# Attention layer: fill products dealt over the steps, output projection in two halves

## The chip, the cores and the metric

The kernel runs on one core of one Trainium2 chip. The metric is the device time of one execution in microseconds (us). The kernel before ran three times, at 1906.16, 1908.15 and 1908.15 us: median 1908.15 us.

## The reference

The reference is a model of four layers on 512 positions of width 1024, all in float32. The change touches only the last mixer, grouped-query attention with a window of 128 positions, 16 query heads and 4 key/value heads of 64 channels, and the residual sum behind it. `hn` and `hk` are two normalised forms of the same `h`.

```python
q = partial_rope((hn @ w_q).reshape(1, 512, 16, 64), pos)
k, v = partial_rope(hk @ w_k, pos), hk @ w_v             # 4 heads
# per kv head (4) and block of 128 queries (4): keys are this block and the one before
s = (q . k) * 64 ** -0.5, masked to the window of 128
m = max(max(s), sink); pr = exp(s - m)
w = pr / (sum(pr) + exp(sink - m)); o = w @ v
h = h + o @ w_o
h = h + square(relu(rmsnorm(h) @ w_up)) @ w_down         # MLP, 4096 wide
h = h + sigmoid(rmsnorm(h) @ w_gate) * (p @ w_proj)      # p: 512 x 256
```

## The kernel before

Every engine has its own written-out program (`pe_*` for TensorE, `dve_*` for VectorE, `act_*` for ScalarE, `pool_*` for GpSimd, `sync` for the queue SP that issues the DMAs). An engine runs its program strictly in order; semaphores tie the programs together. So the order around the change is set by hand, in `pe_att`, `act_att`, `dve_att` and `pool_att`.

All weights come in units of 128 x 1024 floats, 281 of them, in the fixed order `ORDER`. Unit i is loaded into slot i % 3 of `RAW`; ScalarE rounds it to fp32r (`high`, L276, into `WH`), GpSimd takes the remainder (`low`, L280, into `WL`). A product in full precision is three fp32r matmuls: WH by xh, WL by xh and WH by xl, where xh and xl are the rounded activations and their remainder. A unit is thus 24 matmuls of 128 x 128 by 512 (`linear`, L291, matmul on L304; for the projection of p `mm3`, L287 to L289). `high` of unit i waits until TensorE has finished unit i - 3, and `low` waits for `high`; the next fetch into a slot waits for its `low`.

The attention layer goes like this. Key and value units come first (`wk`, `wv`), then query units 0 to 4, each followed by the rotation of the one before it (`pe_rope`, L2012, between VectorE's scaling L410, its sine product L2017, GpSimd's cosine product L2024 and VectorE's sum L2030). Then 18 steps run, n = 0 to 17, with the 16 pairs of a kv head and a block in a pipeline over the engines:

- TensorE: scores of pair n+1 (`pe_scores`, L2073), output of pair n-2 (`pe_out`, L2162), transposes of the weights of pair n-1 (`pe_weights`, L2144).
- VectorE: masked scores and maxima of pair n in two halves (`dve_scores`, L2096 to L2106), the sum of pair n-1 between them (`dve_sum`, L2119, L2121), the remainder of output n-2 (`dve_out`, L417).
- ScalarE: rounding of output n-2 (`act_out`, L413), exponentials of pair n (`act_exp`, L2112, L2114), copy of the transposes of pair n-1 (`act_weights`, L2152).
- GpSimd: the division of pair n-1 (`pool_weights`, L2127).

A pair whose block is the first has 128 keys, the 12 others 256. Buffers tie the steps: the scores of pair n go into the buffer that the transposes of pair n-2 must have left.

Between these, TensorE has other units to do. Query units 5, 6 and 7 stand whole in steps 0, 2 and 4 (`Q_AT`), between the output and the transposes, with their rotation at the end of the step; the two units of the projection of p (`proj1`) stand whole in steps 9 and 12 (`PJ_AT`), behind the transposes. `act_att` and `pool_att` convert the later weights in those steps as well; in `pool_att` the conversion (`lows`) stands ahead of `pool_weights`. p is split in step 8, into `P0h`/`P0l`.

After the 18 steps come the 8 units of the output projection, `wo`: one for each 128 output channels, over all 8 input chunks, as all 16 pairs must be there. VectorE adds each result to H (L428), ScalarE and VectorE form the input of the MLP from it (L413, L348, L421), and the MLP begins.

The 8 PSUM banks go round in one queue (`banks.take`): whoever takes a bank waits until its last user has let go.

Of the kernel before, what the change touches and what calls it, by code (L numbers as in the profile page):

```python
# [9 lines left out]
F32 = mybir.dt.float32  # L10
# [59 lines left out]

# [3 lines left out]
Q_AT = {0: 5, 2: 6, 4: 7}  # L74
PJ_AT = {9: 0, 12: 1}


def att_units():
    out = [("wk", 0, 0), ("wk", 0, 1), ("wv", 0, 0), ("wv", 0, 1)] + [("wq", 0, n) for n in range(5)]
    out += [("wq", 0, n) for n in Q_AT.values()] + [("proj1", 0, h) for h in PJ_AT.values()]  # L80
    return out + [("wo", 0, n) for n in range(8)]
# [58 lines left out]
def program(nc, ctx, known, D):  # L140
# [96 lines left out]
    RP = sb("RP", [128, 4, T], F32, sub)  # L237
    sub.close()
# [52 lines left out]
    def linear(pe, what, xh, xl, chunks, freed_by, ready=None, half=None, first=False):  # L291
# [14 lines left out]
        for n, c in enumerate(chunks):  # L306
# [12 lines left out]
            if half and n == 5:  # L319
                half()  # L320
# [129 lines left out]
    def pe_even(pe):  # L450
# [4 lines left out]
        for n, (kind, c) in enumerate(EVEN):  # L455
            what = even_what(n)
            if kind in "GABFS":
                linear(pe, what, P0h, P0l, range(8), "evac_d", "even" if n == 0 else None,
                       {2: lambda: stat_sums(pe, "even", True), 3: lambda: spread_even(pe)}.get(n), n == 0)
# [18 lines left out]
            elif kind == "K":  # L478
                linear(pe, what, E1h, E1l, range(8), "h", "yb" if c == 0 else None,
                       (lambda: stat_spread(pe, "ln")) if c == 5 else None)  # L480
            else:
                linear(pe, what, E2h, E2l, range(8), "h", "ya" if c == 0 else None)
# [1308 lines left out]
    def p_buf(l, kc):  # L1791
        return RP[:, kc, :] if l else tmp(4 + kc)

    def p_split(l, kc):
        return (P0h, P0l) if l else (P2h, P2l)
# [10 lines left out]
    def pe_proj(pe, l, h):  # L1806
# [4 lines left out]
        for n in range(4):  # L1811
            c = 4 * h + n
            b, before = banks.take(("pj", l, c), "evac_a")
            pe.wait_ge(*at(*before))
            for kc in range(2):
# [3 lines left out]
                last = mm3(pe, b[:, :], wh[:, ws], wl[:, ws], xh[:, kc, :], xl[:, kc, :], kc == 0, kc == 1)  # L1819
            last.then_inc(*inc("unit", what if n == 3 else ("pj", l, c)))  # L1820

    def act_proj(act, l, h):
        for n in range(4):
            c = 4 * h + n
# [355 lines left out]
    def pe_att(pe):  # L2180
# [8 lines left out]
        for n in range(5):  # L2189
# [3 lines left out]
        pe_rope(pe, ("q", 4))  # L2193
        pe_scores(pe, 0)
        for n in range(18):
# [16 lines left out]

    def act_att(act):
# [6 lines left out]
        for n in range(18):  # L2220
            if 1 < n:
                act_out(act, n - 2)
            if n < 16:
                act_exp(act, n)
            if n in Q_AT:
                highs(act, IDX[("wq", 0, Q_AT[n])] + 4)
            if 0 < n < 17:
                act_weights(act, n - 1)
            if n in PJ_AT:
                highs(act, IDX[("proj1", 0, PJ_AT[n])] + 4)  # L2230
                act_proj(act, 1, PJ_AT[n])
            if n == 8:
                act_p(act, 1)
        for n in range(8):
            highs(act, IDX[("wo", 0, n)] + 4)
            norm_in_act(act, "mlp1", n, [("mlp1", P0h, vec("norm_mlp", 8 + n))], ("wo", 0, n))

    def dve_att(dve):
# [9 lines left out]
        for n in range(7):  # L2248
            if n > 1:
                dve_rope_out(dve, ("q", n - 2))  # L2250
            if n < 5:
                dve_rope_in(dve, ("q", n))
            if 0 < n < 6:
                dve_rope_sin(dve, ("q", n - 1))
        for n in range(18):
# [6 lines left out]
            if n in Q_AT:  # L2262
                dve_rope_in(dve, ("q", Q_AT[n]))
            if n > 1:
                dve_out(dve, n - 2)
            if n in Q_AT:
                dve_rope_sin(dve, ("q", Q_AT[n]))
# [300 lines left out]
```

## Time and profile before

| | us |
|---|---|
| median of three runs | 1908.15 |
| the profiled execution, its own time | 1902.84 |
| its span, first to last instruction | 1901.0 |
| TensorE busy with matmuls, whole span | 1776.7 (93%) |
| the steps, from the first scores to the first wo matmul | 161.9, TensorE busy 126.04 |
| the 8 wo units behind them | 43.7, TensorE busy 43.66 |

The rows speak of one profiled execution; the figures of a stretch are in us from the span's start. "PEclk" is the clock that TensorE was granted, 1.00 being the full 2.4 GHz. An idle time in square brackets stands before the instruction, with the one that ended it.

### The profile page before, as it was taken

To read this page: it belongs to the slowest core of one execution; us is meant where nothing else is said; L and a number is where in the kernel's file an instruction comes from. 1 tells how busy PE (TensorE), PEld (TensorE's weight loads), DVE (VectorE), ACT (ScalarE), POOL (GpSimd) and SP (SyncE) were. 2 spreads that over 40 slices of the span, in tenths; PEclk is the share of its full clock that TensorE was granted. 3 is DMA by queue.
4 is the path that set the end of the run, shared out by engine and by line. 5 is a ranking of instruction groups with operands and counts; after the bars stand their busy time and mean duration, and the time that the engine had idled before them with its cause. 6 is when DMAs were issued, how large, how long until landed. Compare 5 with 4: busy or idle time off the path is not lost.

```text
span 1901.0 us, 20872 instructions
## 1 busy us (share of the span) xinstructions
PE 1776.7 (93%) x7994; PEld 1440.6 (76%) x7994; DVE 894.8 (47%) x1297; ACT 760.5 (40%) x1194; POOL 976.5 (51%) x613
## 2 busy tenths in 40 slices
PE   9999988999998889999999999897888999999996
PEld 7887876777777777888888888674456888888885
DVE  3999956676665874622121213723452221212125
ACT  5233324377765553343232323422454432323242
POOL 5869544577555564644444445652234544444462
PEclk9999999999998899999999999897889999999998
DMA  4323213222221233222232222220001222232221
GB/s 160 109 78 111 100 67 102 87 79 89 89 80 48 80 104 106 94 100 93 95 100 100 90 98 97 70 87 25 23 22 46 99 96 93 100 100 93 96 100 45
DMA packets 55107, 164.04 MB, mean 86 GB/s; under 512 B 6368, under 2 KB 14176, under 8 KB 54880
## 3 DMA queue, kind: packets, MB, share of 16 engines
q1 hardware_dynamic: 55008, 162.71, 25.4%
q8 instruction: 64, 1.05, 0.2%
q14 instruction: 35, 0.29, 0.0%
HBM read 156.66 MB, written 6.03 MB: 86 GB/s over the span
## 4 chain that ended last, share of the span: by engine, by line
PE 67%; DVE 11%; issue 8%; ACT 7%; POOL 7%; DMA 0%; SPq 0%; POOLq 0%; DVEq 0%; ACTq 0%
PE B L304 57%; DVE B L587 3%; POOL WL L280 3%; PE B L287 1%; ACT WH L276 1%; PE B L289 1%; PE B L288 1%; PE B L1616 1%; PE B L2162 1%; PE B L1509 1%; PE B L2144 1%; DVE P0l L421 1%; DVE SW L1113 1%; POOL TMP L2127 1%; ACT TMP L2112 1%
## 5 line engine op out<-in xcount | busy, mean ns | idle before, releaser
L280 POOL TENSOR_TENSOR WL<-RAW,WH 128x1024 fp32r<-128x1024 f32 x281 | 682.8, 2432 | 712.7 <-ACT WH L276 712.7
L276 ACT ACTIVATE WH<-RAW 128x1024 fp32r<-128x1024 f32 x281 | 296.8, 1059 | 743.6 <-PE B L304 713.0
L304 PE MATMUL B<-P0h,WH 128*128 128x512 f32 x1128 | 444.1, 394 | 5.9 <-ACT P0h L413 3.9
L304 PE MATMUL B<-P0l,WH 128*128 128x512 f32 x1128 | 437.0, 393 | 1.0 <-DVE P0l L421 1.0
L304 PE MATMUL B<-P0h,WL 128*128 128x512 f32 x1128 | 284.9, 390 | 2.3 <-POOL WL L280 2.3
L304 PEld LDWEIGHTS B<-P0h,WH 128*128 128x128 f32 x1128 | 213.0, 189 | 55.5 <-issue 5.6
L304 PEld LDWEIGHTS B<-P0l,WH 128*128 128x128 f32 x1128 | 213.8, 190 | 46.3 <-DVE P0l L421 1.5
L304 PEld LDWEIGHTS B<-P0h,WL 128*128 128x128 f32 x1128 | 211.9, 188 | 46.6 <-POOL WL L280 2.7
L428 DVE TENSOR_TENSOR H<-H,B 128x512 f32<-128x512 f32 x96 | 65.8, 686 | 318.9 <-PE B L304 318.9
L304 PE MATMUL B<-P1h,WH 128*128 128x512 f32 x512 | 199.7, 390 | 1.4 <-DVE P1l L417 1.4
L304 PE MATMUL B<-P1l,WH 128*128 128x512 f32 x512 | 194.7, 389 | 0.0
L1882 DVE SCALAR_TENSOR_TENSOR TMP<-B,RS 128x512 f32<-128x512 f32 x64 | 44.1, 691 | 258.4 <-PE B L304 244.0
L587 DVE SCALAR_TENSOR_TENSOR B<-UP,VE,B 128x512 f32<-128x512 f32 x232 | 156.5, 750 | 1.6 <-ACT B L531 1.6
L304 PE MATMUL B<-P1h,WL 128*128 128x512 f32 x512 | 131.0, 389 | 0.0
L304 PEld LDWEIGHTS B<-P1h,WH 128*128 128x128 f32 x512 | 96.1, 188 | 22.1 <-DVE P1l L417 2.3
L304 PEld LDWEIGHTS B<-P1h,WL 128*128 128x128 f32 x512 | 96.1, 188 | 19.9
L304 PEld LDWEIGHTS B<-P1l,WH 128*128 128x128 f32 x512 | 96.1, 188 | 19.9
L357 POOL TENSOR_TENSOR ACC<-ACC,TMP 128x512 f32<-128x512 f32 x51 | 74.1, 1453 | 52.7 <-ACT TMP L348 52.5
L304 PE MATMUL B<-P2h,WH 128*128 128x512 f32 x144 | 56.7, 394 | 9.0 <-ACT P2h L413 9.0
L304 PE MATMUL B<-P2l,WH 128*128 128x512 f32 x144 | 54.3, 402 | 0.0
L421 DVE SCALAR_TENSOR_TENSOR P0l<-H,VE,P0h 128x512 fp32r<-128x512 f32 x40 | 46.0, 1161 | 13.6 <-ACT P0h L413 13.6
L2127 POOL TENSOR_SCALAR TMP<-TMP,AS 128x256 f32<-128x256 f32 (+1 forms) x64 | 27.9, 456 | 44.6 <-DVE AS L2121 44.6
(327 smaller groups left out, 2676.5 us busy)
## 6 DMA issues: line engine op xcount, KB each, us to landing
RAW<-in_w SPq DMA_DIRECT2D x281, 512.0 KB, 3.2
H<-in_xT SPq DMA_DIRECT2D x8, 256.0 KB, 4.6
g<-GB SPq DMA_DIRECT2D x8, 256.0 KB, 2.1
GB<-g SPq DMA_DIRECT2D x32, 64.0 KB, 2.0
out<-TMP SPq DMA_DIRECT2D x8, 256.0 KB, 2.1
u<-TMP SPq DMA_DIRECT2D x7, 256.0 KB, 2.0
U<-u SPq DMA_DIRECT2D x28, 64.0 KB, 2.0
SPT<-in_ssm SPq DMA_DIRECT2D x1, 1040.0 KB, 5.7
```

What stands on the lines that cost most here:

```text
L276: act.activation(WH[:, i % NS, :], RAW[:, i % NR, :], ACT.Copy).then_inc(*inc("w_hi", i))
L280: pool.tensor_tensor(WL[:, i % NS, :], RAW[:, i % NR, :], WH[:, i % NS, :].bitcast(F32), ALU.subtract).then_inc(*inc("w_lo", i))
L287: pe.matmul(out, wh, xh, start=start, stop=False)
L288: pe.matmul(out, wl, xh, start=False, stop=False)
L289: return pe.matmul(out, wh, xl, start=False, stop=stop)
L304: return pe.matmul(b[:, :], w[:, ws[c]], x[:, c, :], start=start, stop=stop)
L357: pool.tensor_tensor(ACC[:, :], ACC[:, :], tmp(c % 2), ALU.add).then_inc(*inc("acc", (k, c)))
L421: dve.scalar_tensor_tensor(dst, src, g, hi.bitcast(F32), ALU.mult, ALU.subtract).then_inc(*inc("x_lo", (k, c)))
L428: dve.tensor_tensor(H[:, n, :], H[:, n, :], banks.bank[what][:, :], ALU.add).then_inc(*inc("h", key))
L587: dve.scalar_tensor_tensor(chunk(c) if j == 30 else CB[c % 2][:, :], UP[:, c, j:j + T], w, CB[c % 2][:, :], ALU.mult, ALU.add).then_inc(*i ...
L1882: dve.scalar_tensor_tensor(mlp_tmp(q, c), banks.bank[what][:, :], 0.0, rs(f"mlp{l}"), ALU.max, ALU.mult).then_inc(*inc("evac_d", what))
L2127: pool.tensor_scalar(s_head(n, h), s_head(n, h), st[:, 16 + h:17 + h], 1.0, ALU.mult, ALU.mult).then_inc(*inc("att_w", (n, h)))
```

## The change

Query units 5 to 7, the projection of p and a first half of the output projection become one stream of 216 matmuls (`pe_fill`), dealt out over the 18 steps: 24 in step 0, none behind; then 4 behind the output and 8 behind the transposes in each step, 2 and 4 in steps 8 and 9, and 0 and 12 in step 17. The output projection is cut by its input: `woa` holds input chunks 0 to 3 (kv heads 0 and 1, pairs 0 to 7), `wob` chunks 4 to 7, in 4 units each with two output chunks per unit. `woa` is in the stream; `wob` follows the steps. VectorE adds to H twice per chunk. The stream has two PSUM banks of its own (`fbanks`), the pairs keep six. In ScalarE's program the exponentials now come ahead of the rounding of the output, and in GpSimd's the division ahead of the conversion of weights. p is loaded earlier, into a buffer of its own (`PB`), and split in step 2.

```diff
+FILL = {0: (24, 0), 8: (2, 4), 9: (2, 4), 17: (0, 12)}
+FILLED = {0: ("wq", 0, 5), 2: ("wq", 0, 6), 4: ("wq", 0, 7), 6: ("proj1", 0, 0), 9: ("proj1", 0, 1),
+          11: ("woa", 0, 0), 13: ("woa", 0, 1), 15: ("woa", 0, 2)}
+ROT_AT = {0: 4, 1: 5, 3: 6, 5: 7}
+PJ_END = {5: (0, 1), 6: (2, 3), 7: (4, 5), 8: (6,), 9: (7,)}
...
@@ def pe_att
-        for n in range(5):
+        for n in range(4):
             linear(pe, ("wq", 0, n), P0h, P0l, range(8), "evac_d")
             if n:
                 pe_rope(pe, ("q", n - 1))
-        pe_rope(pe, ("q", 4))
+        linear(pe, ("wq", 0, 4), P0h, P0l, range(8), "evac_d", between={3: lambda: pe_rope(pe, ("q", 3))})
+        for _ in range(2):
+            fbanks.queue.append(banks.queue.popleft())
+        products = pe_fill(pe)
+
+        def fill(n, after):
+            for _ in range(FILL.get(n, (4, 8))[after]):
+                next(products)
         pe_scores(pe, 0)
         for n in range(18):
             if n < 15:
                 pe_scores(pe, n + 1)
             if n > 1:
                 pe_out(pe, n - 2)
-            if n in Q_AT:
-                linear(pe, ("wq", 0, Q_AT[n]), P0h, P0l, range(8), "evac_d")
+            fill(n, 0)
             if 0 < n < 17:
                 pe_weights(pe, n - 1)
-            if n in PJ_AT:
-                pe_proj(pe, 1, PJ_AT[n])
-            if n in Q_AT:
-                pe_rope(pe, ("q", Q_AT[n]))
-        for n in range(8):
-            if n == 0:
-                pe.wait_ge(*at("x_lo", ("o", 15)))
-            linear(pe, ("wo", 0, n), P1h, P1l, range(8), "h")
+            fill(n, 1)
+            if n in ROT_AT:
+                pe_rope(pe, ("q", ROT_AT[n]))
+        banks.queue.extend(fbanks.queue)
+        for j in range(4):
+            for _ in pe_wo(pe, "wob", j, banks):
+                pass
...
+    def pe_fill(pe):
+        for n in (5, 6, 7):
+            yield from pe_queries(pe, n)
+        for h in range(2):
+            yield from pe_proj(pe, 1, h, fbanks)
+        for j in range(4):
+            yield from pe_wo(pe, "woa", j, fbanks)
...
+    def pe_wo(pe, part, j, pool):
...
+        pe.wait_ge(*at("w_lo", IDX[what]))
+        if j == 0:
+            pe.wait_ge(*at("x_lo", ("o", 15 if first else 7)))
+        for m in range(2):
+            n = 2 * j + m
+            b, before = pool.take((part, n), ("h", wo_sum(part, n)))
+            pe.wait_ge(*at(*before))
+            for kc in range(4):
...
@@ def act_att
         for n in range(18):
+            act_proj(act, 1, PJ_END.get(n - 1, ()))
+            if n - 1 in FILLED:
+                highs(act, IDX[FILLED[n - 1]] + 4)
+            if n < 16:
+                act_exp(act, n)
             if 1 < n:
                 act_out(act, n - 2)
-            if n < 16:
-                act_exp(act, n)
-            if n in Q_AT:
-                highs(act, IDX[("wq", 0, Q_AT[n])] + 4)
             if 0 < n < 17:
                 act_weights(act, n - 1)
...
-            if n == 8:
+            if n == 2:
                 act_p(act, 1)
...
@@ def dve_att
             if n < 16:
                 dve_scores(dve, n, 1)
-            if n in Q_AT:
-                dve_rope_in(dve, ("q", Q_AT[n]))
+            if n in ROT_AT and n:
+                dve_rope_in(dve, ("q", ROT_AT[n]))
+            if n - 1 in ROT_AT:
+                dve_rope_sin(dve, ("q", ROT_AT[n - 1]))
+                dve_rope_out(dve, ("q", ROT_AT[n - 1]))
+            if n > 10:
+                dve_wo(dve, "woa", n - 11)
             if n > 1:
                 dve_out(dve, n - 2)
...
-            if n == 8:
+            if n == 2:
                 dve_p(dve, 1)
+        dve_wo(dve, "woa", 7)
         for n in range(9):
             if n < 8:
-                add_to_h(dve, ("wo", 0, n), n, ("wo", 0, n), ("ple", 0, n))
+                dve_wo(dve, "wob", n)
...
@@ def pool_att
         for n in range(18):
-            if n in Q_AT:
-                lows(pool, IDX[("wq", 0, Q_AT[n])] + 4)
+            if n and n - 1 in ROT_AT:
+                pool_rope_cos(pool, ("q", ROT_AT[n - 1]))
             if 0 < n < 17:
                 pool_weights(pool, n - 1)
-            if n in PJ_AT:
-                lows(pool, IDX[("proj1", 0, PJ_AT[n])] + 4)
-            if n in Q_AT:
-                pool_rope_cos(pool, ("q", Q_AT[n]))
+            if n - 1 in FILLED:
+                lows(pool, IDX[FILLED[n - 1]] + 4)
...
@@ def sync
-            elif i == IDX[("wq", 0, 7)] + 5:
-                sp.wait_ge(*at("rope", ("q", 7)))
+            elif i == IDX[("wq", 0, 1)] + 2:
+                sp.wait_ge(*at("unit", ("wv", 0, 1)))
```

`FILL` gives the matmuls behind the output and behind the transposes, 4 and 8 where a step is not named. `FILLED` names the unit that the stream has finished by the end of a step, and so when ScalarE and GpSimd convert the next one. `ROT_AT` is the step at whose end a query unit is rotated, `PJ_END` the projection results that the stream has finished in a step.

## Rows read from the trace of the kernel before

**Rows 1.** Clock slices of the page: granted clock in tenths, 40 slices of the span.
```profile
PEclk9999999999998899999999999897889999999998
```

**Rows 2.** Windows: stretch, length, busy us (x instructions) of PE, PEld, DVE, ACT, POOL; clock.
```profile
1278.90:1440.80 161.90, 126.04 (x423) 73.43 (x422) 72.23 (x174) 67.50 (x204) 47.62 (x75) 0.83 0.07 23
1440.80:1484.50 43.70, 43.66 (x193) 36.15 (x194) 8.79 (x13) 15.38 (x21) 24.39 (x13) 1.00 0.23 75
```

**Rows 3.** Waits of TensorE in the steps: total us, times, longest.
```profile
PE B L2144 <- POOL TMP L2127: 9.9, 4, 4.2
```

**Rows 4.** Timelines of ACT, POOL and PE behind query unit 6: start, us, instruction.
```profile
1317.32 1.06 ACT L276 ACTIVATE WH<-RAW 128x1024 fp32r<-128x1024 f32 x1 [3.95 <-PE B L304]
...
1318.45 2.34 POOL L280 TENSOR_TENSOR WL<-RAW,WH 128x1024 fp32r<-128x1024 f32 x1 [13.92 <-ACT WH L276]
1320.77 1.85 POOL L2127 TENSOR_SCALAR TMP<-TMP,AS 128x256 f32<-128x256 f32 x4
...
1321.40 2.60 PE L2144 MATMUL B<-CO,TMP 128*128 128x128 f32 x8 [4.18 <-POOL TMP L2127]
```

**Rows 5.** Timeline of PE, one step without other units, at full clock.
```profile
1370.55 1.09 PE L2144 MATMUL B<-CO,TMP 128*128 128x128 f32 x8
1371.57 1.99 PE L2073 MATMUL B<-KT,Q 64*128 64x256 f32 x8
1374.22 1.90 PE L2162 MATMUL B<-TMP,V 128*64 128x512 f32 x4 [0.65 <-ACT TMP L2152]
```

**Rows 6.** Timeline of PE: output and scores of a pair with 128 keys.
```profile
1363.94 1.04 PE L2162 MATMUL B<-TMP,V 128*64 128x512 f32 x2 [0.81 <-ACT TMP L2152]
...
1366.42 1.16 PE L2073 MATMUL B<-KT,Q 64*128 64x128 f32 x8
```

**Rows 7.** Timeline of PE: a rotation; the instructions before and behind a projection unit.
```profile
1270.44 1.02 PE L2012 MATMUL B<-RP,CO 128*128 128x512 f32 x2
...
1409.01 1.09 PE L2144 MATMUL B<-CO,TMP 128*128 128x128 f32 x8
...
1415.53 1.99 PE L2073 MATMUL B<-KT,Q 64*128 64x256 f32 x8
```

**Rows 8.** Timeline of PE: into the steps, and a spell at the lower clock.
```profile
1276.78 2.19 PE L2012 MATMUL B<-RP,CO 128*128 128x512 f32 x4
...
1283.93 4.60 PE L2073 MATMUL B<-KT,Q 64*128 64x128 f32 x12 [4.32 <-DVE Q L2030]
...
1396.09 2.17 PE L2144 MATMUL B<-CO,TMP 128*128 128x128 f32 x8 [1.27 <-POOL TMP L2127]
...
1400.19 3.67 PE L2162 MATMUL B<-TMP,V 128*64 128x512 f32 x4
```

**Rows 9.** Timelines of DVE, then ACT: one round of VectorE and ScalarE.
```profile
1366.59 0.69 DVE L2096 SCALAR_TENSOR_TENSOR TMP<-B,CO 128x512 f32<-128x512 f32 x1
...
1368.28 0.68 DVE L2096 SCALAR_TENSOR_TENSOR TMP<-B,CO 128x512 f32<-128x512 f32 x1
...
1370.23 0.15 DVE L2106 TENSOR_TENSOR AS<-VE,AS 128x4 f32<-128x4 f32 x1
1371.28 0.69 DVE L417 TENSOR_TENSOR P1l<-B,P1h 64x512 fp32r<-64x512 f32 x1 [0.90 <-ACT P1h L413]
...
1370.66 0.59 ACT L413 ACTIVATE P1h<-B 64x512 fp32r<-64x512 f32 x1 [1.59 <-PE B L2162]
1371.28 0.51 ACT L2112 ACTIVATE TMP<-TMP,AS 128x256 f32<-128x256 f32 x1
...
1373.26 0.19 ACT L2114 ACTIVATE AS<-AS 128x4 f32<-128x4 f32 x1
```

**Rows 10.** Timelines of POOL and DVE: the sum of a rotation beside GpSimd, and alone.
```profile
1280.76 2.48 POOL L2024 TENSOR_TENSOR RP<-RP,RO 128x512 f32<-128x512 f32 x2
...
1282.05 1.73 DVE L2030 TENSOR_TENSOR Q<-RP 128x512 f32<-128x512 f32 x1 [3.52 <-POOL RP L2024]
...
1284.49 0.69 DVE L2030 TENSOR_TENSOR Q<-RP 128x512 f32<-128x512 f32 x1
```

More of the change, by code:

```diff
@@ L318, in linear @@
                 product(wh, xl, c)
-            if half and n == 5:
-                half()
+            if n in between:
+                between[n]()
         if first:
@@ L1812, in pe_proj @@
             c = 4 * h + n
-            b, before = banks.take(("pj", l, c), "evac_a")
+            b, before = pool.take(("pj", l, c), "evac_a")
             pe.wait_ge(*at(*before))
@@ new lines, in pe_att @@
+            if n in ROT_AT:
[4 more added lines that the diff above has]
+                pass
+    fbanks = Banks([])
+    fbanks.bank = banks.bank
+    def pe_fill(pe):
[5 more added lines that the diff above has]
+            yield from pe_wo(pe, "woa", j, fbanks)
@@ new lines, in pe_queries @@
+    def pe_queries(pe, n):
+        what = ("wq", 0, n)
+        wh, wl = weights(IDX[what])
+        b, before = fbanks.take(what, "evac_d")
+        pe.wait_ge(*at(*before))
+        pe.wait_ge(*at("w_hi", IDX[what]))
+        for c in range(8):
+            ws = slice(128 * c, 128 * c + 128)
+            pe.matmul(b[:, :], wh[:, ws], P0h[:, c, :], start=c == 0, stop=False)
+            yield
+            pe.matmul(b[:, :], wh[:, ws], P0l[:, c, :], start=False, stop=False)
+            yield
+        pe.wait_ge(*at("w_lo", IDX[what]))
+        for c in range(8):
+            last = pe.matmul(b[:, :], wl[:, 128 * c:128 * c + 128], P0h[:, c, :], start=False, stop=c == 7)
+            if c == 7:
+                last.then_inc(*inc("unit", what))
+            yield
@@ new lines, in wo_unit, with wo_sum @@
+    def wo_unit(part, n):
+        return (part, 0, n // 2) if n % 2 else (part, "half", n // 2)
+    def wo_sum(part, n):
+        return ("wo", 0, n) if part == "wob" else (part, n)
+    def pe_wo(pe, part, j, pool):
+        what = (part, 0, j)
+        wh, wl = weights(IDX[what])
+        first = 4 if part == "wob" else 0
+        pe.wait_ge(*at("w_lo", IDX[what]))
+        if j == 0:
[3 more added lines that the diff above has]
+            b, before = pool.take((part, n), ("h", wo_sum(part, n)))
+            pe.wait_ge(*at(*before))
+            for kc in range(4):
+                ws = slice((4 * m + kc) * 128, (4 * m + kc) * 128 + 128)
+                pe.matmul(b[:, :], wh[:, ws], P1h[:, first + kc, :], start=kc == 0, stop=False)
+                yield
+                pe.matmul(b[:, :], wl[:, ws], P1h[:, first + kc, :], start=False, stop=False)
+                yield
+                last = pe.matmul(b[:, :], wh[:, ws], P1l[:, first + kc, :], start=False, stop=kc == 3)
+                if kc == 3:
+                    last.then_inc(*inc("unit", wo_unit(part, n)))
+                yield
@@ L2213, in act_att, with dve_wo @@
+    def dve_wo(dve, part, n):
+        dve.wait_ge(*at("unit", wo_unit(part, n)))
+        dve.wait_ge(*at("h", wo_sum("woa", n) if part == "wob" else ("ple", 0, n)))
+        dve.tensor_tensor(H[:, n, :], H[:, n, :], banks.bank[part, n][:, :], ALU.add).then_inc(
+            *inc("h", wo_sum(part, n)))
     def act_att(act):
@@ L2437, in unit_tiles @@
         return [(8 + kc, 2 * b + m) for m in range(2) for kc in range(4)]
+    if name in ("woa", "wob"):
+        return [(4 * (name == "wob") + kc, 2 * b + m) for m in range(2) for kc in range(4)]
     if name == "wv":
```

76 lines of the change are left out of this document (41 added, 35 removed).

## The prediction

> **What bounds the kernel now.** I read the page's clock slices first. They hold 9 but for a few [rows 1], and the lowest, slices 28 to 30 of 40 with 7, 8 and 8, lie where attention is. The windows say how much is there [rows 2]: the steps take 161.9 us with TensorE busy for 126.0 of them at a mean granted clock of 0.83; the 8 wo units behind them take 43.7 us, all busy, at 1.00. So 35.9 us of the steps are idle. The waits of TensorE [rows 3] name GpSimd's division L2127 first, 9.9 us in 4 waits. The timelines show how such a wait comes about [rows 4]. Query unit 6 stands whole in step 2. ScalarE can round the next unit only when it ends (1317.32), GpSimd takes the remainder at 1318.45, and the division that the transposes want stands behind that in GpSimd's program, until 1320.77. TensorE has meanwhile idled 4.18 us, and the transposes then run at the lower clock, 2.60 us where the same 8 take 1.09 [rows 4, 5]. In steps without a unit TensorE waits too, 0.65 us for a copy [rows 5]. TensorE's own work in the steps is therefore the floor, and everything above it is latency between engines and the clock that the gaps cost.
>
> **TensorE's work at full clock.** In a run of instructions the last 0.07 us of each lies under the next (1370.55 + 1.09 against 1371.57), so I take that off. A step of 256 keys: transposes 1.02, scores 1.92, output 1.83, in sum 4.77 us [rows 5]. A pair of 128 keys: scores 1.09, output 0.97 [rows 6], half of the transposes 0.51, in sum 2.57. Twelve of the one and four of the other: 57.2 + 10.3 = 67.5 us. A unit of 24 fp32r matmuls is 43.7 / 8 = 5.46 us [rows 2]; the projection unit, from 1409.01 + 1.02 to 1415.53, took 5.50 [rows 7], so going into a burst of them costs 0.04 more. A rotation is 0.95 [rows 7].
>
> Before, the steps hold 67.5 + 5 x 5.46 + 3 x 0.95 = 97.7 us of work in 161.9. The missing 64.2 are the 35.9 idle and, by difference, 28.3 of lower clock.
>
> **After, part by part.** The stream has 216 matmuls, 9 units: 49.1 us. It comes in 34 bursts: 1.4. Four rotations stand in the steps (query units 4 to 7): 3.8. `wob` is 4 units: 21.8. With the pairs' 67.5 that is 143.6 us from the first scores to the start of the MLP. The number of wo matmuls is unchanged, 192; VectorE gets 8 additions of some 0.69 more.
>
> The first scores now come 0.95 after unit 4, since rotation 3 has gone into the middle of that unit: 1276.78 + 0.95 = 1277.7, where before two rotations stood there [rows 8]. The 4.32 us wait on VectorE's rotation sum in front of the next scores [rows 8] goes: pairs 0 to 7 need only query units 0 to 3, the last rotated 3.6 us before, which covers cosine (2.48 / 2 = 1.24) and sum (0.69) [rows 10]. Without any stall the MLP would start at 1277.7 + 143.6 = 1421.3, against 1484.5.
>
> **Whether the other engines keep up.** A full step of TensorE is 4.77 + 12 x 0.2275 + 0.08 = 7.58 us. The ring that could be slower goes through VectorE and ScalarE: first half of the scores until the second (1366.59 to 1368.28, 1.69), second half to its last instruction's end (1370.38, 2.10), exponentials (1371.28 to 1373.45, 2.17), rounding of the output until VectorE starts on it (0.62), and that 0.69, with some 0.05 [rows 9]: 7.3 us. So TensorE is the slower one by 0.3 us a step. Within the step VectorE's new wo addition and the rotation work (each 0.69, at most 1.4 in one step) come while ScalarE does exponentials and rounding, a gap of 2.8 us, and cost nothing; were that cover gone, each would lengthen the ring by 0.69. GpSimd has the division (1.85) and in every second step a remainder (2.34) [rows 4], in three a cosine: 5.4 at most, and the remainder now stands behind the division. TensorE wants a pair's transposes 2.74 us after the output starts, and the division is over more than 2 us before that. ScalarE's conversions of weights wait only for units finished in the step before and come ahead of the exponentials, which VectorE releases some 2 us into the step; two projection copies (0.59 each, the row of the rounding) and one conversion (1.06) just fit.
>
> Banks: with six of them and 4 or 5 takes a step, the output n-2 wants the bank whose second-half scores VectorE must have read. That gives VectorE 1.3 us of slack against TensorE. The stream's two banks come back a step ahead.
>
> Fetches: the load of p now stands in SP's queue behind the fetch of query unit 3 and waits for the last value unit. The next fetch is held until then, some 4 us; it is needed two units of 5.46 later. No cost. The rest of SP's queue has one wait fewer.
>
> **Stalls that I expect.** (1) Step 2 has the split of p: ScalarE two copies of about 0.59, VectorE two remainders of about 0.69 behind the output's [rows 9], by the rows of the same operations on 64 partitions. VectorE comes to the next scores about 2.2 us late, beyond its slack; following it through, TensorE loses 2.0 us. Bounds: 0, if slack of the first steps is larger, and 4, all four instructions in the open. (2) At the end no scores are left to fill steps 15 to 17; the output of pair 14 waits for the copy behind the last exponentials, about 1.5 us (bounds 0 and 4). (3) The clock. Before, a 1.27 us gap was followed by a spell of half speed, in which the transposes took 2.17 and the output 3.67 against 1.09 and 1.90 [rows 8, 5]: 2.9 us lost in those two rows. One such spell more, for stall 1: 3.3, an estimate from these with part of the scores between them (bounds 0 and 8, two spells and more). Sum 6.8.
>
> Sum: 1421.3 + 6.8 = 1428.1, so 1484.5 - 1428.1 = 56.4 us gained. Behind it nothing changes: per output chunk ScalarE has 1.9 us, GpSimd one addition and half a remainder, VectorE 1.4, all under the 2.73 us of a wob chunk, and the MLP's first unit covers the last one's chain as it does now. The profiled execution would go from 1902.84 to 1846.4 (span 1844.6). The median of the runs lies 5.3 above the profiled one, so I put the same 56.4 to it: 1908.15 - 56.4 = 1851.8, call it 1852.
>
> **A rule weighed.** VectorE's sum of a rotation took 0.69 us alone and 1.73 while GpSimd's cosine product ran beside it [rows 10]. In the change these sums come while GpSimd is in its division. The Trainium skill, GPSIMD Engine Reference, section Specifications, says that GpSimd's access to SBUF is shared with VectorE and that they contend when a VectorE instruction has two SBUF inputs, which this sum has. By the quiet row the four sums in the steps cost 2.8 us of VectorE, by the rule with the slow row 6.9. As they lie in the gap of 2.8 us, the forecast is the same by either; it would show in rival one.
>
> **Rivals.**
> *One: the ring of VectorE and ScalarE becomes the bound.* For it: it is only 0.3 us shorter than TensorE's step, and instructions stretch beside GpSimd [rows 10]. Against: the ring's rows come from steps where all engines ran. If the two hidden instructions come into the open the ring is 7.3 + 1.4 = 8.7 us, 1.1 over TensorE's step; over 15 steps 16 us: 1868.
>
> *Two: the clock stays as it was in the steps.* For it: between 1396 and 1405 TensorE was hardly idle and still slow [rows 8]. Against: where the pairs ran without long gaps it was at 1.00 with more idle than the new steps have [rows 5]. If the former loss of 28.3 comes back in place of my 3.3: 1852 + 25 = 1877.
>
> *Three, slower than before: the lower clock for all of the mixed steps.* The place is the 18 steps, the mechanism that short float32 products of 64 rows or columns between short bursts don't bring the clock back. 67.5 + 49.1 + 3.8 + 1.4 = 121.8 us at the ratio 3.67 / 1.90 [rows 8, 5] are 113 us more: 1965. It decides against the change from the point where half of the steps' work (56 of 113) runs at the lower clock. Against it: slow spells end within ten microseconds in the trace, with fewer matmuls in them.
>
> *Four: no difference.* The stream's matmuls only replace idle time that is then lost elsewhere, in a wait that I don't see, such as the first wo half waiting on pair 7's remainder. Step 10 begins a whole step after that remainder, so there is little for it. 1908.
>
> **Chances.** Forecast 0.71 (its own range, by the bounds of its three stalls, 1845 to 1861), rival one 0.17, two 0.07, three 0.03, four 0.02. A measurement of this kernel tells no less than about 0.2%, 4 us, from no change. Faster by more than that 0.95, within it 0.02, slower 0.03. The range goes from 1843, the forecast without any stall with 2 us for another session, to 1872, which takes in rival one.
>
> **What would show it.** In the steps' window TensorE's busy share over 95% and a clock of at least 0.97, and about 128 us from first scores to first wob matmul in place of 161.9; the wo window at 21.8 in place of 43.7; the next pair's transposes following the fill with no wait on GpSimd L2127; one wait of about 2 us behind step 2 and one in steps 15 and 16. Rival one would show as a wait of TensorE for VectorE's scores L2096 in every step and a period near 8.7; rivals two and three in the clock column alone. A gain under 40 us would make the prediction wrong, and so would a gain of over 65, for then the floor of TensorE's work is not as I sum it.

## The result, and the profile after

| | before | after |
|---|---|---|
| median, us | 1907.2 of 4 runs (1906.16 to 1908.15) | 1856.49 of 4 runs (1850.77 to 1859.78) |
| the profiled execution, and its span | 1902.84, 1901.0 | 1854.97, 1853.2 |
| first scores to the MLP's first matmul | 1278.90 to 1484.49: 205.59 | 1283.12 to 1435.33: 152.21 |
| idle of TensorE in it | 35.9 | 5.05 |

The ratio of the medians is 0.9733, interval 0.9712 to 0.9754: the change takes 2.7% off. The forecast was 1852 and the range 1843 to 1872.

The page of after, its span, TensorE's busy time and the clock slices; [rows 1] answer to the last:

```profile
span 1853.2 us, 20888 instructions
...
PE 1759.0 (95%) x7994; PEld 1432.1 (77%) x7994; DVE 912.2 (49%) x1305; ACT 761.6 (41%) x1194; POOL 981.5 (53%) x613
...
PEclk9999998999998899999999999989999999999998
```

The 7 and the two 8s of slices 28 to 30 have become 9s. The 8 in slice 27 lies in the key units ahead of the steps, and the one in slice 7 far ahead of the attention layer. Next the windows of after: the steps, then the `wob` units, with the columns of [rows 2], whose two stretches they answer to. The third row is the steps about the first wait.

```profile
1283.10:1413.50 130.40, 125.35 (x521) 80.25 (x521) 80.40 (x181) 72.51 (x208) 55.51 (x77) 0.99 0.11 37
1413.50:1435.30 21.80, 21.80 (x98) 18.05 (x97) 12.84 (x14) 12.65 (x18) 17.00 (x9) 1.00 0.22 73
1300.00:1317.00 17.00, 15.40 (x61) 9.28 (x61) 11.13 (x29) 9.82 (x28) 6.80 (x11) 0.90 0.14 50
```

The steps hold 98 matmul records more than before and last 31.5 us less, at a clock of 0.99 where it was 0.83. What is left of idle time stands in the waits of TensorE (total us, times, longest), against 9.9 us for the division alone in [rows 3]:

```profile
PE B L2177 <- DVE TMP L2111: 3.0, 4, 0.9
PE B L2088 <- DVE TMP L2111: 1.7, 3, 0.8
PE B L2177 <- DVE P1l L425: 0.4, 1, 0.4
```

None is for GpSimd. L2177 is the output and L2088 the scores, and both wait for VectorE's masked scores L2111. The timeline of TensorE puts them into steps 3, 7 and 11 (steps are named by the output of pair n - 2 in them):

```profile
1307.05 0.71 PE L2088 MATMUL B<-KT,Q 64*128 64x128 f32 x4 [0.71 <-DVE TMP L2111]
1308.65 2.63 PE L2177 MATMUL B<-TMP,V 128*64 128x512 f32 x4 [0.89 <-DVE TMP L2111]
...
1342.09 1.93 PE L2177 MATMUL B<-TMP,V 128*64 128x512 f32 x4 [0.88 <-DVE TMP L2111]
...
1368.14 0.71 PE L2088 MATMUL B<-KT,Q 64*128 64x128 f32 x4 [0.81 <-DVE TMP L2111]
1369.73 1.93 PE L2177 MATMUL B<-TMP,V 128*64 128x512 f32 x4 [0.89 <-DVE TMP L2111]
...
1403.18 1.90 PE L2177 MATMUL B<-TMP,V 128*64 128x512 f32 x4 [0.39 <-DVE P1l L425]
```

With 0.31 in step 6 and 0.17 in step 7 that is 1.60, 0.31, 1.05, 1.70 and 0.39: 5.05 us. The output behind the first wait takes 2.63 in place of 1.93, and its window has the clock 0.90: a spell of the lower level, 1.2 GHz.

**Why step 11 waits.** Steps 8 and 9 have only 6 matmuls of the stream. The outputs of pairs 6, 7 and 8 on TensorE, then the last instruction of a round of VectorE (L2121) for pairs 8 to 11:

```profile
1349.71 1.93 PE L2177 MATMUL B<-TMP,V 128*64 128x512 f32 x4
...
1355.95 1.93 PE L2177 MATMUL B<-TMP,V 128*64 128x512 f32 x4
...
1361.78 1.07 PE L2177 MATMUL B<-TMP,V 128*64 128x512 f32 x2
```
```profile
1349.63 0.15 DVE L2121 TENSOR_TENSOR AS<-VE,AS 128x4 f32<-128x4 f32 x1
...
1356.61 0.15 DVE L2121 TENSOR_TENSOR AS<-VE,AS 128x4 f32<-128x4 f32 x1
...
1363.92 0.15 DVE L2121 TENSOR_TENSOR AS<-VE,AS 128x4 f32<-128x4 f32 x1
...
1370.96 0.15 DVE L2121 TENSOR_TENSOR AS<-VE,AS 128x4 f32<-128x4 f32 x1
```

VectorE's rounds last 6.98, 7.31 and 7.04: the ring of the prediction (scores and maxima on VectorE, exponentials and rounding on ScalarE, remainder on VectorE), whose full size was put at 7.3. TensorE's steps are 6.24, 5.83 and, without its waits, 1369.73 - 1361.78 - 1.70 = 6.25. Over the three the ring needs 21.33 and TensorE 18.32; the difference of 3.01, less the slack of 1.3 at which the prediction put the six banks (an estimate, not measured by itself), is 1.7, which is what step 11 waits.

**A small instruction held by GpSimd.** VectorE's timeline, then GpSimd's, in step 5. L2120 is a `tensor_scalar` on 128 x 4 values, which is 0.17 to 0.44 us long elsewhere; L288 is GpSimd's remainder of a weight unit:

```profile
1326.01 2.29 DVE L2120 TENSOR_SCALAR AS<-AS 128x4 f32<-128x4 f32 x1
1328.22 0.15 DVE L2121 TENSOR_TENSOR AS<-VE,AS 128x4 f32<-128x4 f32 x1
```
```profile
1325.94 2.35 POOL L288 TENSOR_TENSOR WL<-RAW,WH 128x1024 fp32r<-128x1024 f32 x1
```

The one ends at 1328.30, the other at 1328.29. The exponentials wait for the small instructions, so the ring was 2.1 us longer this once. Steps 6 and 7 then wait 1.4 us. I put that down to the held instruction; no run with the exponentials first is without one there, so it is not shown by itself.

**Behind the steps.** GpSimd in the `wob` stretch, then TensorE's sums of squares (L383) for the norm of the MLP:

```profile
1428.74 3.18 POOL L365 TENSOR_TENSOR ACC<-ACC,TMP 128x512 f32<-128x512 f32 x2
1431.87 2.86 POOL L288 TENSOR_TENSOR WL<-RAW,WH 128x1024 fp32r<-128x1024 f32 x1
1434.69 3.44 POOL L365 TENSOR_TENSOR ACC<-ACC,TMP 128x512 f32<-128x512 f32 x2
1438.10 2.84 POOL L288 TENSOR_TENSOR WL<-RAW,WH 128x1024 fp32r<-128x1024 f32 x1
1440.90 1.26 POOL L365 TENSOR_TENSOR ACC<-ACC,TMP 128x512 f32<-128x512 f32 x1
```
```profile
1442.31 1.02 PE L383 MATMUL B<-MEAN,ACC 128*128 128x1 f32 x8 [1.37 <-POOL ACC L365]
```

For two chunks GpSimd needs 3.18 + 2.86 = 6.0 us, while TensorE takes 5.45. It falls behind and TensorE waits 1.37 for its last addition.

### The profile page after: what moved, and what is told of

Its sections match the earlier page's. It is cut to its first block, busy times and chain, and to the rows that moved or that the text cites. A ratio compares the mean times of both kernels' runs of the same rounds, so it can differ in the third digit from the quotient of the medians.

```text
span 1853.2 us, 20888 instructions
## 1 busy us (share of the span) xinstructions
PE 1759.0 (95%) x7994; PEld 1432.1 (77%) x7994; DVE 912.2 (49%) x1305; ACT 761.6 (41%) x1194; POOL 981.5 (53%) x613
## 3 DMA queue, kind: packets, MB, share of 16 engines
q8 instruction: 64, 1.05, 0.2%
## 4 chain that ended last, share of the span: by engine, by line
PE 70%; DVE 12%; ACT 6%; POOL 6%; issue 5%; DMA 0%; SPq 0%; DVEq 0%; POOLq 0%; ACTq 0%
PE B L312 57%; DVE B L595 3%; POOL WL L288 2%; PE B L2177 1%; ACT WH L284 1%; PE B L2088 1%; DVE P0l L429 1%; PE B L295 1%; PE B L1624 1%; PE B L296 1%; PE B L297 1%; PE B L1517 1%; POOL ACC L365 1%; PE B L2159 1%; DVE SW L1121 1%
## 5 line engine op out<-in xcount | busy, mean ns | idle before, releaser
L288 POOL TENSOR_TENSOR WL<-RAW,WH 128x1024 fp32r<-128x1024 f32 x281 | 684.0, 2437 | 634.0 <-ACT WH L284 634.0
L312 PE MATMUL B<-P0h,WH 128*128 128x512 f32 x1104 | 433.2, 392 | 5.7 <-ACT P0h L421 4.0
L312 PE MATMUL B<-P0l,WH 128*128 128x512 f32 x1104 | 426.5, 392 | 1.0 <-DVE P0l L429 1.0
L312 PEld LDWEIGHTS B<-P0l,WH 128*128 128x128 f32 x1104 | 208.4, 189 | 45.4 <-DVE P0l L429 1.5
L436 DVE TENSOR_TENSOR H<-H,B 128x512 f32<-128x512 f32 x88 | 60.3, 686 | 284.3 <-PE B L312 284.3
L312 PE MATMUL B<-P1h,WH 128*128 128x512 f32 x448 | 174.7, 390 | 0.0
L312 PE MATMUL B<-P1l,WH 128*128 128x512 f32 x448 | 169.8, 389 | 0.0
L312 PE MATMUL B<-P1h,WL 128*128 128x512 f32 x448 | 115.2, 389 | 0.0
L365 POOL TENSOR_TENSOR ACC<-ACC,TMP 128x512 f32<-128x512 f32 x51 | 75.2, 1475 | 53.1 <-ACT TMP L356 52.6
L312 PEld LDWEIGHTS B<-P1h,WL 128*128 128x128 f32 x448 | 84.1, 188 | 17.5
L312 PEld LDWEIGHTS B<-P1l,WH 128*128 128x128 f32 x448 | 84.1, 188 | 17.4
L312 PEld LDWEIGHTS B<-P1h,WH 128*128 128x128 f32 x448 | 84.1, 188 | 17.4
```

Of the source, the lines that this page charges most:

```text
L288: pool.tensor_tensor(WL[:, i % NS, :], RAW[:, i % NR, :], WH[:, i % NS, :].bitcast(F32), ALU.subtract).then_inc(*inc("w_lo", i))
L312: return pe.matmul(b[:, :], w[:, ws[c]], x[:, c, :], start=start, stop=stop)
L365: pool.tensor_tensor(ACC[:, :], ACC[:, :], tmp(c % 2), ALU.add).then_inc(*inc("acc", (k, c)))
L436: dve.tensor_tensor(H[:, n, :], H[:, n, :], banks.bank[what][:, :], ALU.add).then_inc(*inc("h", key))
```

## The experiments

The ratios are to the kernel before, run on the same chip. "Stretch" is the time from the first scores to the MLP's first matmul, 152.21 in the profile of after. A second profile of the same kernel gave 157.31 (the last experiment), so a difference of 5 us between two stretches can be chance. Every kernel here is the whole change but for what is named. The diffs show the deciding lines, and "..." marks what is left out. First come parts of the change, then the parts whose cost the profile disputes.

**The dealing without half of `wo`.** Query and projection units are dealt out, `wo` stays whole behind the steps; 2 and 2 matmuls in a step from step 5 on. The change's orders in ScalarE and GpSimd, its two banks for the stream and its early split of p are kept.

```diff
-FILL = {0: (24, 0), 8: (2, 4), 9: (2, 4), 17: (0, 12)}
+FILL = {0: (24, 0), 1: (4, 8), 2: (4, 8), 3: (4, 8), 4: (4, 8), 17: (0, 0)}   # others (2, 2)
...
@@ pe_att
-        for j in range(4):
-            for _ in pe_wo(pe, "wob", j, banks):
-                pass
+        for n in range(8):
...
+            linear(pe, ("wo", 0, n), P1h, P1l, range(8), "h")
...
```

> One part of the change alone: query units 5 to 7 and the projection of p are dealt out over the steps (12 matmuls in steps 1 to 4, then 4 a step), while the output projection keeps its 8 whole units behind the steps. All work is done. Stretch read: first scores to the MLP's first matmul, 205.6 us before and 152.2 with the whole change. Theory (TensorE's work is the floor, and the ring through VectorE and ScalarE of 7.3 us the next one): from step 5 on TensorE has 4.77 + 4 x 0.23 = 5.7 us a step, so the ring binds at about 7.2 and 6.7 for the pairs of 128 keys; steps about 120, wo 43.7, together about 164 us, time about 1868. Rival (the gain is the half of wo that moved, 21.8 us, and a little of dealing): the stretch keeps about 185 us, time about 1887.

Measured: 1867.22, ratio 0.9799 [0.9783, 0.9816], stretch 169.86. Two thirds of what the change takes off the stretch is here, by the dealing and the new orders together: 205.6 - 169.9 = 35.7 of 53.4 us. No run has the new orders without the dealing. The stretch is 6 us above what was expected. Steps with four matmuls of the stream are shorter than the ring, and at the end nothing covers it. Two waits of the timeline of TensorE (L2176 is the output):

```profile
1390.78 3.42 PE L2176 MATMUL B<-TMP,V 128*64 128x512 f32 x4 [2.38 <-ACT TMP L2166]
...
1398.07 1.90 PE L2176 MATMUL B<-TMP,V 128*64 128x512 f32 x4 [1.74 <-DVE P1l L424]
```

**All that moves, in whole units.** The same work as in the change, but each unit in one burst of 24; the additions of `woa` to H come one step later.

```diff
+FILL = {0: (24, 0), 2: (24, 0), 4: (24, 0), 7: (0, 24), 9: (0, 24), 11: (0, 24), 13: (0, 24), 15: (0, 24),
+        17: (0, 24)}                                                           # others (0, 0)
...
```

> The other part alone: everything is moved as in the change, the first half of the output projection too, but each unit stands whole: 24 matmuls at once in steps 0, 2 and 4 ahead of the transposes, in steps 7, 9, 11, 13, 15 and 17 behind them. The additions of the first half to H come one step later. All work is done. Theory (even dealing matters, since a step with no fill waits for the ring and a step with 24 is TensorE's): steps alternate between about 7.2 and 10.3 us, the steps come to about 148 us instead of 130, the stretch to about 170, time about 1875. Rival (only the amount of work put into the steps matters, slack of a step carries over): stretch within 4 us of 152, time about 1857.

Measured: 1873.72, ratio 0.983 [0.9814, 0.9847], stretch 173.85. TensorE waits in many steps, up to 2.94 us; 14.0 of the 17.1 us of its waits in the steps are for L2112, the masked scores. So moving half of `wo` into the steps brings little unless it is dealt evenly: dealt, the same matmuls need 21.6 us less by the first profile of the change, 16.5 by the second.

**The output projection cut, but not moved.** The first experiment, with `woa` and `wob` both behind the steps.

```diff
-            linear(pe, ("wo", 0, n), P1h, P1l, range(8), "h")
+        for part in ("woa", "wob"):
+            for j in range(4):
+                for _ in pe_wo(pe, part, j, banks):
+                    pass
...
```

> As the kernel that only deals out queries and projection, but the output projection is cut in two by its input there, and both halves follow the steps; nothing of it is dealt out. It gives the price of the cut by itself. Theory (same 192 matmuls; 8 more additions on VectorE, and the second half gives results every 2.73 us, too fast for GpSimd beside VectorE): steps as in that kernel, wo 43.6, the wait of 1.4 us for the sums of squares appears, which that kernel doesn't have; time within 2 us above 1867. Rival (the cut costs more, by the additions or by waits for banks): over 4 us above it.

Measured: 1870.37, ratio 0.9798 [0.9781, 0.9814] against 0.9799 of the first experiment, stretch 166.71. In us that is 3 above the first experiment and was expected within 2, but the kernel before ran 2.5 us longer there too, and the ratios are equal. The sums of squares, which do not wait in the first experiment (1454.56), wait here:

```profile
1450.91 1.14 PE L382 MATMUL B<-MEAN,ACC 128*128 128x1 f32 x8 [1.40 <-POOL ACC L364]
```

With `wo` whole, a finished chunk comes every 5.46 us, with `wob` every 2.73. The cut gains something too: in the first experiment TensorE waits 1.41 us ahead of `wo` for the remainder of the last output (1405.24), and here it does not, as `woa` needs only pairs 0 to 7. The two about cancel, and the runs show neither a gain nor a loss of the cut by itself.

**p split ahead of the steps.** This tests stall (1).

```diff
@@ act_att
-            if n == 2:
-                act_p(act, 1)
+        act_p(act, 1)
         for n in range(18):
...
@@ dve_att
+            if n == 0:
+                dve_p(dve, 1)
...
-            if n == 2:
-                dve_p(dve, 1)
```

> The whole change, but p is split ahead of the exponentials of step 0 and in VectorE's step 0 instead of in step 2, where both engines idle. Theory (the split makes VectorE late for the scores of pair 3, TensorE waits 1.6 us in step 3 and then has a spell of half clock that costs about 1.5): the stretch 152.2 falls by about 3 us, and no wait of TensorE is left in step 3. Rival (the wait in step 3 comes from the ring of VectorE and ScalarE itself, as those in steps 7 and 11 do, with 1.1 and 1.7 us): the wait in step 3 stays at 1 us or more and the stretch falls by under 1.

Measured: 1855.67, ratio 0.9731 [0.9703, 0.9758], stretch 153.88. The wait of step 3 is gone, so it was the split of p. But nothing was won, since another came in step 11, as the timeline of this kernel shows for VectorE, GpSimd, ScalarE and TensorE:

```profile
1360.04 2.45 DVE L2121 TENSOR_TENSOR AS<-VE,AS 128x4 f32<-128x4 f32 x1
1360.08 2.40 POOL L288 TENSOR_TENSOR WL<-RAW,WH 128x1024 fp32r<-128x1024 f32 x1
...
1362.53 0.51 ACT L2127 ACTIVATE TMP<-TMP,AS 128x256 f32<-128x256 f32 x1 [4.75 <-DVE AS L2121]
...
1366.54 0.71 PE L2088 MATMUL B<-KT,Q 64*128 64x128 f32 x4 [3.10 <-DVE TMP L2111]
```

L2121, 0.15 us long elsewhere, ends with GpSimd's L288 (1362.49 and 1362.48), and the wait that the light steps cause anyway is 3.10 + 0.89 in place of 1.70.

**ScalarE rounds the output ahead of the exponentials,** as in the kernel before. If the ring is what TensorE waits for, this shortens it: VectorE's next round then has its remainder L425 without the exponentials before it.

```diff
@@ act_att
-            if n < 16:
-                act_exp(act, n)
             if 1 < n:
                 act_out(act, n - 2)
+            if n < 16:
+                act_exp(act, n)
```

> The whole change, but ScalarE rounds the output of pair n-2 ahead of the exponentials of pair n, as in the kernel before. Theory (the order in the change ties VectorE's next scores to the end of the exponentials, a ring of 7.3 us that shows as waits in steps 3, 7 and 11; with the rounding first that ring is cut, and the exponentials start about 2 us later with room to spare): stretch shorter by 2 to 3 us, waits of TensorE for the scores L2111 gone in steps 7 and 11. Rival (the exponentials' later start pushes the sum, the division and the copy of the transposes past TensorE's wish, as before the change): TensorE waits for GpSimd's division or ScalarE's copy in most full steps, stretch longer by 10 us or more.

Measured: 1849.56, ratio 0.9703 [0.9685, 0.9721], stretch 149.04. Only the wait of step 3 is left, 1.68 + 0.89 in place of 1.60; why it grew was not looked into. VectorE's round from L2121 of pair 10 to that of pair 11 now follows TensorE:

```profile
1359.27 0.15 DVE L2121 TENSOR_TENSOR AS<-VE,AS 128x4 f32<-128x4 f32 x1
...
1361.22 0.69 DVE L2111 SCALAR_TENSOR_TENSOR TMP<-B,CO 128x512 f32<-128x512 f32 x1 [0.76 <-PE B L2159]
...
1364.78 0.15 DVE L2121 TENSOR_TENSOR AS<-VE,AS 128x4 f32<-128x4 f32 x1
```

It takes 5.51 us, 0.76 of them waiting for TensorE. L2121 and L2120 were held here too (2.40 at 1307.84, 2.29 at 1324.07), and no step waits behind them: the shorter ring has room for it. So putting the exponentials ahead of the rounding was no gain of the change: with the rounding first the stretch is 3.2 us shorter than in the first profile of the change and 8.3 shorter than in the second.

**GpSimd's conversion kept off the small instructions,** on top of the last one.

```diff
@@ pool_att
             if n - 1 in FILLED:
+                if n < 16:
+                    pool.wait_ge(*at("att_d", (n, "sink_m")))
                 lows(pool, IDX[FILLED[n - 1]] + 4)
```

> As the kernel that rounds first, and GpSimd's conversion of weights (L288, two inputs in SBUF) waits in each step until VectorE has done the small operations behind the maxima. Theory (a small VectorE operation that falls beside L288 lasts until L288 ends: 2.29 and 2.40 us in place of 0.17 in the kernel that rounds first, in steps 5 and 3): no such operation over 1 us from step 1 on, the waits of TensorE in step 3 fall from 2.57 to about 1 us (the rest is the split of p), stretch from 149.0 to about 147. Rival (the step 3 wait is all the split of p, and the long small operations lie in slack): wait in step 3 stays at 2 us or more and the stretch within 0.5 of 149.

Measured: 1850.52, ratio 0.9696 [0.9679, 0.9713], stretch 149.05. From step 1 on none of these small instructions is over 1 us long, and TensorE's wait in step 3 is the same 1.68 + 0.89. The theory written there missed and its rival held: with the rounding in front, held instructions lie in slack.

**GpSimd's order undone:** the conversion again ahead of the division.

```diff
@@ pool_att
-            if 0 < n < 17:
-                pool_weights(pool, n - 1)
             if n - 1 in FILLED:
                 lows(pool, IDX[FILLED[n - 1]] + 4)
+            if 0 < n < 17:
+                pool_weights(pool, n - 1)
```

> The whole change with one part undone: in GpSimd's program the conversion of weights stands ahead of the division again. Theory (the transposes want the division 2.7 us after the output starts; with the conversion ahead of it, which waits for ScalarE and takes 2.4, it is over about 1 us too late in the 8 steps that have one): waits of TensorE for GpSimd's division of 0.5 to 1.5 us in most of these steps, stretch longer by 5 to 10 us than 152.2. Rival (the division has slack enough in either order): no wait for the division, stretch within 1 us of 152.2.

Measured: 1863.06, ratio 0.9767 [0.9751, 0.9784], stretch 165.26, 13.1 longer than the first profile of the change and 8.0 longer than the second. The wait of [rows 3] is back, in three places of the eight. GpSimd, then TensorE, at the first:

```profile
1291.31 2.37 POOL L288 TENSOR_TENSOR WL<-RAW,WH 128x1024 fp32r<-128x1024 f32 x1
1293.67 1.85 POOL L2142 TENSOR_SCALAR TMP<-TMP,AS 128x128 f32<-128x128 f32 x4
```
```profile
1294.62 1.29 PE L2159 MATMUL B<-CO,TMP 128*128 128x128 f32 x4 [1.57 <-POOL TMP L2142]
```

The waits for the division are 3.7 us; neither profile of the change has one. They were expected in most of the eight steps. All waits are 9.2 us against 5.05 and 7.6. The rest of the difference can't be read from waits; it is lower clock by difference, 0.96 in the steps against 0.99 and 0.97. The runs do not show a price: this kernel's 1863.06 is 6.6 us above the first runs of the change and level with the second, 1863.52.

**Everything that the waits point to.** Rounding first, p early, the wait of GpSimd, and the last conversion but one of the `wob` stretch moved behind the last addition, where the last stands already:

```diff
@@ pool_att, behind the steps
             add_square(pool, "mlp1", n)
-            if n % 2 == 0:
+            if n % 2 == 0 and n < 6:
                 lows(pool, IDX[("wob", 0, n // 2)] + 4)
+        lows(pool, IDX[("wob", 0, 3)] + 4)
```

> The kernel without the lock, with p split ahead of the steps and with GpSimd's last conversion (of the MLP's third unit) behind the last addition of squares instead of ahead of it. Theory: no wait of TensorE over 1 us from the first scores on; stretch about 145.5 (143.6 of TensorE's work by the prediction, and 2 for going in and out of bursts); the 1.4 us wait for the sums of squares behind the MLP's first unit gone; time about 1845. Rival (the wait for the sums is GpSimd's additions lengthened by VectorE, 1.6 to 1.75 us in place of 1.3, in all chunks, so that one conversion less doesn't make it good): a wait of 1 us or more stays there.

Measured: 1843.45 (1837.45 to 1845.94), ratio 0.9654 [0.9635, 0.9673], stretch 144.45. It is the best of all, 0.8% under the first runs of the change and 1.1% under the second. Its windows, steps and `wob`, have TensorE busy without a gap at full clock, and the sums of squares no longer wait:

```profile
1280.90:1403.60 122.70, 122.70 (x521) 79.42 (x521) 78.51 (x181) 71.57 (x208) 56.12 (x77) 1.00 0.12 40
1403.60:1425.40 21.80, 21.80 (x98) 18.05 (x97) 12.91 (x14) 12.64 (x18) 17.00 (x9) 1.00 0.21 73
```
```profile
1430.87 0.95 PE L383 MATMUL B<-MEAN,ACC 128*128 128x1 f32 x8
```

**The same without GpSimd's wait,** to see if that part does anything.

```diff
@@ pool_att
-                if n < 16:
-                    pool.wait_ge(*at("att_d", (n, "sink_m")))
```

> The last kernel (rounding first, p split ahead of the steps, last conversion behind the last addition) without GpSimd's wait for VectorE's small operations. Theory (with the rounding first, VectorE has room in every step, and a small operation held for 2.3 us costs nothing): one or two small operations of over 2 us in the steps, no wait of TensorE over 0.5 us, stretch within 0.5 of 144.45. Rival (as in the kernel with p split early and the exponentials first, where the held operation at 1360.04 cost TensorE 3.1 and 0.9 us): a wait of 1 us or more in the step of such an operation, stretch longer by 2 to 5 us.

Measured: 1844.3, ratio 0.9668 [0.9655, 0.9682], stretch 144.48, no wait. L2120 was held again (2.29 at 1319.47) and cost nothing, so that wait can be left out.

**The change once more,** not altered, in another session.

> The change itself once more, unaltered, to see what of its profile repeats. Theory (the waits of TensorE in steps 3, 7 and 11 and behind the MLP's first unit are set by the order of the programs; what comes 3.5 us later than in the kernel before by the first key unit, 1212.75 against 1209.24, is not): the same waits within 0.3 us each, stretch 152.2 within 1.5; the first key unit anywhere between 1208 and 1213. Rival (the late start is a property of the change): first key unit again at 1212 or later.

Measured: 1863.52 (1854.2 to 1865.81), ratio 0.9763 [0.974, 0.9786], stretch 157.31. The key units begin at 1210.45, as the theory had it; the stretch missed its expectation by 5 us. The waits of the first profile are all there. Step 16's, 0.39 in the first, is 1.00 (1405.98), and there are two more, 0.89 (1347.52) and 1.05 (1398.68): 7.6 us in all against 5.05. L2121 was held three times beside L288, at 1307.61, 1341.04 and 1392.66, where the first profile has no such case; the two new waits come behind the second and the third. The first of them, on VectorE and on GpSimd:

```profile
1307.61 2.40 DVE L2121 TENSOR_TENSOR AS<-VE,AS 128x4 f32<-128x4 f32 x1
```
```profile
1307.63 2.36 POOL L288 TENSOR_TENSOR WL<-RAW,WH 128x1024 fp32r<-128x1024 f32 x1
```

The same place in the first profile, VectorE, then GpSimd:

```profile
1309.87 0.15 DVE L2121 TENSOR_TENSOR AS<-VE,AS 128x4 f32<-128x4 f32 x1
```
```profile
1308.09 1.85 POOL L2142 TENSOR_SCALAR TMP<-TMP,AS 128x256 f32<-128x256 f32 x4 [5.52 <-DVE AS L2136]
1309.91 2.37 POOL L288 TENSOR_TENSOR WL<-RAW,WH 128x1024 fp32r<-128x1024 f32 x1
```

This is a race that the programs set up. GpSimd's division starts at VectorE's reciprocal L2136, and L288 stands right behind it; from the same reciprocal VectorE goes on to L2121. In both profiles L2121 comes 2.04 or 2.05 us after the reciprocal's start, and L288 2.07 to 2.09. Each profile has four such meetings, with L288 0.02 to 0.04 us behind: in the first none is held, in the second three. Which one happens can't be told from the recorded starts, as 0.03 is there with and without a hold. That fits the change's spread, 1850.8 to 1865.8 over both sessions, against 1837.5 to 1845.9 for the two versions above in which held instructions cost nothing, whose stretches were 144.45 and 144.48; that it is the whole of the spread was not shown.

## Why the prediction was right, and where it was off

**The mechanism was right.** The division's wait is gone and the clock is back. The dealing can't be left out (1873.72 us in bursts). With GpSimd's order undone the waits for the division come back, 3.7 us, but the runs can't tell that kernel from the change's second ones. The floor of TensorE's work was put at 143.6 us; the kernel with no wait at all has 144.45. `wob` took 21.80 as forecast, and a full step 1384.95 - 1377.34 = 7.61 by its outputs, against 7.58. The steps to the first `wob` matmul took 130.4 and not 128, with TensorE busy for 96% of them. Rivals two to four did not come: the clock is 0.99.

**The gain in the profile was 47.8 us (spans 1901.0 and 1853.2) and not 56.4.** By the steps of the prediction:

| step | predicted | measured |
|---|---|---|
| TensorE's work to the MLP | 143.6 | 144.45 |
| stall (1), split of p | 2.0 | 1.60 |
| stall (2), the end | 1.5 | 0.39 |
| waits in steps 6, 7 and 11 | 0 | 3.06 |
| stall (3), lower clock | 3.3 | 2.7, by difference |
| sum, the stretch | 150.4 | 152.2 |
| first scores | 1277.7 | 1283.12 |
| behind the stretch | 0 | 1.4 |

1.8 + 5.4 + 1.4 make the 8.6 us. That the stretch came so near is in part luck: the stalls were put at 6.8 us and came to 7.8, but 3.1 of these are waits that the prediction had at nothing, and stalls (1) and (2) were 1.5 smaller than forecast. The same kernel's second profile had 157.31, so the stretch is known to some 5 us only.

"So TensorE is the slower one by 0.3 us a step" failed. It was worked out for the full step and holds there; in the steps with 6 matmuls of the stream, and where a 128-key pair makes TensorE's part shorter, the ring is the slower one by up to 1.5 us. `FILL` had said so. That is rival one in part: the ring decides in three places (steps 6, 7 and 11), not in all 15 steps, and costs 3.1 us and not 16; 1.4 of them are put down to a held instruction. Its other half, instructions that GpSimd stretches, came too, but not where it was looked for. The four rotation sums in the steps took 0.69 each, as by the quiet row of [rows 10]. The ones that were held are instructions of 128 x 4 values on the ring itself, which the prediction had priced at nothing.

"Behind it nothing changes" failed by 1.4 us. GpSimd's budget per chunk was said to be under 2.73 us, "one addition and half a remainder". By the durations alone that is 1.26 + 1.2 = 2.5. Beside VectorE's instructions it is 3.0, the rows of which stand above.

The first scores came 5.4 us late. Of this, 3.5 are there when the first key unit begins (1212.75 against 1209.24), in code that the change leaves alone. The eleven profiles taken with that code have it between 1208.7 and 1212.8, and the second run of the change at 1210.45, so this does not belong to the change. The other 1.9 lie in the key units, where the clock stayed down longer: 0.88 in the 20 us from 1230 in after, 0.98 in the same 20 us (from 1226.5) before. The kernel with the cut `wo` kept the time of before there, nine others that of after. Why was not settled.

The median of after lies 1.5 us above its profiled execution, where that of before lay 5.3 above in the runs that the prediction had. That took 3.8 us back, so the forecast of 1852 missed by 4.5 only. This too is luck: the change's second runs have the median 1863.52, 11.5 above the forecast.

## What to carry to other kernels

Set the work that fills a gap against the period of the ring of the other engines step by step, not for the mean step: a step with half the fill is shorter than the ring, and the engine pays as soon as its slack in buffers is used up. Before adding fill, look for an order that shortens the ring; here a rounding ahead of the exponentials took 3.2 us off the stretch (8.3 by the second profile), and it also took the price off the instructions held by GpSimd. When a stretch is made shorter, every engine's work in it needs a new budget, by durations taken beside the other engines. Profile the same kernel twice before a difference of a few us between two kernels is explained: here two profiles of one kernel lay 5 us apart.

## What the hardware showed that was not expected

A VectorE instruction on 128 x 4 values can take as long as the GpSimd instruction that it meets. L2121, with two inputs in SBUF, took 2.40 to 2.45 beside L288 and 0.15 without it; L2120, a `tensor_scalar` with one, took 2.29 in place of 0.17. All of them end within 0.05 us of GpSimd's instruction. The Trainium skill has this: SBUF — State Buffer, section Who interferes with whom, says that GpSimd and a VectorE instruction with two SBUF inputs, or a `tensor_scalar` in a mode that uses both ports, share a port pair, and that whichever starts first has it for the whole instruction while the other is blocked. The trace agrees on the held ones. It agrees for the division too, which is four instructions of about 0.46 us (1.85 in all): in both profiles of the change L2120 took 0.17 wherever GpSimd was idle and 0.42 to 0.44 wherever it was dividing. Who starts first can't be checked from recorded starts where they lie close: L2121 at 1307.61 was held by an instruction whose recorded start is 0.02 later, and the one at 1309.87, 0.04 ahead, was not held. The prediction took the price of that sharing from one long instruction (0.69 to 1.73), and by that rule it should have been asked of each instruction on the ring, short ones first.

GpSimd loses as well: two additions L365 took 3.18 to 3.44 in the `wob` stretch, 1.26 to one alone, and L288 2.86 in place of 2.40.
